# Expert matrices of a mixture-of-experts stage: two chunks of 704 columns in place of four of 352

## What is computed

```python
g, u = jnp.split(x @ w_gu[ex], 2, axis=-1)      # w_gu[ex]: 1024 x (2 * 1408)
y = (jax.nn.silu(g) * u) @ w_dn[ex]             # w_dn[ex]: 1408 x 1024
```

## Time and profile before

| | |
|---|---|
| median of three runs (lowest, highest) | 2723.92 us (2721.8, 2724.9) |
| the profiled execution, its own time | 2721.46 us |
| its span in the trace | 2719.4 us |
| PE busy over the span | 2486.5 us (91%) |
| DVE, ACT busy | 1607.8 us (59%), 1391.2 us (51%) |
| TensorE clock granted, mean | 0.96 of full |
| data moved | 472.23 MB, mean 174 GB/s |

### The profile page before, as it was taken

One profiled execution on the slowest core, in us unless ns is written; L12 is line 12 of the kernel. 1 busy time (PEld: TensorE's weight loads), 2 busy tenths in 40 slices (PEclk: granted clock), 3 DMA queues, 4 the chain that ended last, 5 costly groups with the idle time before them and its releaser, 6 DMA issues. The chain is left out here.

```text
span 2719.4 us, 52138 instructions
## 1 busy us (share of the span) xinstructions
PE 2486.5 (91%) x19059; PEld 2166.9 (80%) x19059; DVE 1607.8 (59%) x2330; ACT 1391.2 (51%) x2117; POOL 395.6 (15%) x571
## 2 busy tenths in 40 slices
PE   6998969999889999899799788888999999999993
PEld 4887958778578888788677788777999999999992
DVE  3255566665752232223311688547888888888885
ACT  4225655554323333212222566417888788787873
POOL 1133122221141000011200343042000000000002
PEclk8998989999999999999899899888999999999996
DMA  7530000000541222223254000319999999999994
GB/s 271 203 127 3 18 5 3 3 3 3 197 157 47 77 73 74 77 78 124 79 214 147 31 16 13 120 50 342 381 388 380 387 380 382 383 377 385 376 383 190
DMA packets 262845, 472.23 MB, mean 174 GB/s; under 512 B 29436, under 2 KB 202108, under 8 KB 256548
## 3 DMA queue, kind: packets, MB, share of 16 engines
q1 hardware_dynamic: 255200, 445.69, 46.5%
q0 software_dynamic: 4416, 14.70, 1.4%
q10 hardware_dynamic: 3076, 9.71, 0.9%
HBM read 453.54 MB, written 16.48 MB: 173 GB/s over the span
## 5 line engine op out<-in xcount | busy, mean ns | idle before, releaser
L3379 DVE TENSOR_TENSOR m_lo<-m_raw,m_hi 128x1408 fp32r<-128x1408 f32 (+1 forms) x459 | 648.4, 1457 | 64.8 <-ACT m_hi L3238 62.5
L3238 ACT ACTIVATE m_hi<-m_raw 128x1408 fp32r<-128x1408 f32 (+1 forms) x459 | 548.6, 1246 | 41.8 <-DMA m_raw<-moe_w_gu 27.3
L195 DVE TENSOR_TENSOR w_lo<-w_raw,w_hi 128x1024 fp32r<-128x1024 f32 (+1 forms) x132 | 162.1, 1231 | 485.3 <-ACT w_hi L190 484.7
L213 PE MATMUL acc<-w_hi,h_hi 128*128 128x512 f32 (+1 forms) x1120 | 431.9, 386 | 18.0 <-PEq L2798 9.4
L215 PE MATMUL acc<-w_hi,h_lo 128*128 128x512 f32 (+1 forms) x1120 | 424.9, 379 | 0.0
L214 PE MATMUL acc<-w_lo,h_hi 128*128 128x512 f32 (+1 forms) x1120 | 424.7, 379 | 0.0
L190 ACT ACTIVATE w_hi<-w_raw 128x1024 fp32r<-128x1024 f32 (+1 forms) x134 | 135.0, 1014 | 457.2 <-PE acc L215 401.9
L213 PEld LDWEIGHTS acc<-w_hi,h_hi 128*128 128x128 f32 x1120 | 213.1, 190 | 79.1 <-issue 33.8
L215 PEld LDWEIGHTS acc<-w_hi,h_lo 128*128 128x128 f32 x1120 | 212.9, 190 | 34.5
L214 PEld LDWEIGHTS acc<-w_lo,h_hi 128*128 128x128 f32 x1120 | 213.3, 190 | 32.6
L3156 PE MATMUL p_gates<-m_hi,x_hi 128*128 128x352 f32 x544 | 181.7, 334 | 5.0 <-issue 5.0
(11 more groups left out here) (407 smaller groups left out, 4959.8 us busy)
## 6 DMA issues: line engine op xcount, KB each, us to landing
m_raw<-moe_w_gu SPq DMA_DIRECT2D x544, 352.0 KB
m_raw<-moe_w_dn SPq DMA_DIRECT2D x187, 512.0 KB
ada_w<-ada_w SPq DMA_DIRECT2D x40, 1024.0 KB, 4.9
w_raw<-ffn_w_gu SPq DMA_DIRECT2D x88, 256.0 KB, 2.9
w_raw<-w_in_o SPq DMA_DIRECT2D x24, 512.0 KB, 5.7
w_raw<-ffn_w_dn SPq DMA_DIRECT2D x22, 512.0 KB, 3.6
w_raw<-w_in_e SPq DMA_DIRECT2D x28, 384.0 KB, 5.0
scratch_y_slots<-y_slot ACTq DMA_DIRECT2D x18, 512.0 KB, 6.3
```

Source lines behind the costliest of these rows:

```text
L195: eng.tensor_tensor(lo, self.raw_of(c, k), hi, ALU.subtract).then_inc(self.lo.sem, 1)
L213: eng.matmul(out, hi, whi[:, b, :], start=first, stop=False)
L3238: a.activation(whi[:, u % MSPLIT, 0:size(u)], raw[:, s, 0:size(u)], ACT.Copy).then_inc(s_hi.sem, 1)
L3379: dve.tensor_tensor(wlo[:, u % MSPLIT, 0:n], raw[:, u % MRAW, 0:n], whi[:, u % MSPLIT, 0:n], ALU.subtract).then_inc(s_lo.sem, 1)
```

## The change

The gate and up matrices are read in CH = 2 chunks of ECH = 704 columns. A unit is no longer gates and ups of the same columns, but gates alone or ups alone: four units of gates, then four of ups, for each chunk. The 704 columns are two pieces `q` of 352, each in its own bank, so both banks of an accumulator now belong to one chunk. A piece of a load is 704 consecutive columns (2816 bytes) in place of two runs of 352 (1408 bytes). Number of units, elements in a unit, number and width of matmuls stay.

Silu and product are done twice in a visit, on 704 columns: silu behind units 7 and 15, product behind units 11 and 19. PE waits for the silu before it begins the next chunk's gates, and for the product before its ups. The steps that hang behind units move: `turn_a` to units 10, 11, 19 and 20, AT_PART_A to (14, 15, 21, 22), AT_PART_X from 21 to 19. `turn_x` stays behind unit 16.

```diff
-ECH = 352
+ECH = 2 * 352
...
-    GU, DN = CH * KU, D_EXPERT // P
+    GU, DN = CH * 2 * KU, D_EXPERT // P
...
-    X_USES, A_USES = (3, 4), (0, 1, 2, 5)
-    AT_Y, AT_SILU, AT_PART_A, AT_PART_X = 4, (8, 12, 16, 20), (11, 15, 19, 23), 21
+    X_USES, A_USES = (2, 3), (0, 1, 4, 5)
+    AT_Y, AT_SILU, AT_ACT, AT_PART_A, AT_PART_X = 4, (7, 15), (11, 19), (14, 15, 21, 22), 19
...
+        def chunk_of(u):
+            c, r = divmod(u, 2 * KU)
+            return c, *divmod(r, KU)
...
-                            src = wgu[bass.ds(e, 1), :, 2 * k + b, :, c * ECH:(c + 1) * ECH].rearrange("e p h n -> p (e h) n")
-                            sp.dma_start(gu(raw, u)[:, b], src).then_inc(landed[s].sem, 16)
+                            src = wgu[bass.ds(e, 1), :, 2 * k + b, half, c * ECH:(c + 1) * ECH].rearrange("e p n -> p (e n)")
+                            sp.dma_start(gu(raw, u)[:, b].rearrange("p q n -> p (q n)"), src).then_inc(landed[s].sem, 16)
...
-                pe.wait_ge(s_act.sem, s_act.at(tile * CH + (c + 1)))
+                pe.wait_ge(s_act.sem, s_act.at(tile * CH + (c // 2 + 1)))
...
-                        if k == 0:
-
-                            pe.wait_ge(s_act.sem, s_act.at(tile * CH + (c - 1)))
+                        if k == 0 and half == 0:
+
+                            pe.wait_ge(s_silu.sem, s_silu.at(tile * CH + c))
+                        elif k == 0:
+
+                            pe.wait_ge(s_act.sem, s_act.at(tile * CH + c))
...
-                                pe.matmul(acc[:, c % 2, 0:ECH], xh[:, j, :], h[:, b, half, :], start=start, stop=False)
+                                pe.matmul(acc[:, q, 0:ECH // 2], xh[:, j, :], h[:, b, q, :], start=start, stop=False)
...
-                    if u in (7, 11, 15):
-                        turn_a(tile, (u - 7) // 4)
+                    if u in (10, 11):
+                        turn_a(tile, u - 10)
...
-                    if u == 19:
-                        turn_a(tile, 3)
+                    if u in (19, 20):
+                        turn_a(tile, u - 17)
...
-                        a.wait_ge(s_used.sem, s_used.at(tile * NU + 4 * (c + 1)))
+                        a.wait_ge(s_used.sem, s_used.at(tile * NU + (2 * KU * c + KU)))
...
-                        a.activation(silu[:], pG[:, c % 2, 0:ECH], ACT.Silu).then_inc(s_silu.sem, 1)
+                        a.activation(silu[:].rearrange("p (q n) -> p q n", q=2), pG[:, :, 0:ECH // 2], ACT.Silu).then_inc(s_silu.sem, 1)
...
-                    if u in AT_SILU:
-                        c = AT_SILU.index(u)
+                    if u in AT_ACT:
+                        c = AT_ACT.index(u)
                         dve.wait_ge(s_silu.sem, s_silu.at(tile * CH + (c + 1)))
-                        dve.tensor_tensor(act[:, c * ECH:(c + 1) * ECH], silu[:], pU[:, c % 2, 0:ECH], ALU.mult).then_inc(s_act.sem, 1)
+                        dve.wait_ge(s_used.sem, s_used.at(tile * NU + 2 * KU * (c + 1)))
+                        dve.tensor_tensor(act[:, c * ECH:(c + 1) * ECH].rearrange("p (q n) -> p q n", q=2), silu[:].rearrange("p (q n) -> p q n", q=2),
+                                          pU[:, :, 0:ECH // 2], ALU.mult).then_inc(s_act.sem, 1)
```

More of the change, by code:

```diff
@@ L304, in _ @@
             pe.sem_inc(K.sig("m_act").sem, 2)
+            pe.sem_inc(K.sig("m_silu").sem, 1)
             pe.sem_inc(K.sig("m_y").sem, 1)
@@ L320, in prime @@
     K.sig("m_act").base += 2
+    K.sig("m_silu").base += 1
     K.sig("m_y").base += 1
@@ L2955, in tail_stage @@
     CH, KU = D_EXPERT // ECH, J // 2
-    GU, DN = CH * KU, D_EXPERT // P
+    GU, DN = CH * 2 * KU, D_EXPERT // P
     NU = GU + DN
-    NTURN = CH + 2
     TA = ((0, 2), (2, 5), (5, 8), (8, 11))
-    X_USES, A_USES = (3, 4), (0, 1, 2, 5)
-    AT_Y, AT_SILU, AT_PART_A, AT_PART_X = 4, (8, 12, 16, 20), (11, 15, 19, 23), 21
+    NTURN = len(TA) + 2
+    X_USES, A_USES = (2, 3), (0, 1, 4, 5)
+    AT_Y, AT_SILU, AT_ACT, AT_PART_A, AT_PART_X = 4, (7, 15), (11, 19), (14, 15, 21, 22), 19
     assert NU % MRAW == 0 and NU % MSPLIT == 0
@@ L3010, in tail_stage @@
         idx = K.sb(ctx, "slot_tokens", [P, SLOT_TILES + 1], I32)
-        K.sb(ctx, "gap", [P, 1000])
+        K.sb(ctx, "gap", [P, 1000 - ECH // 2])
         tok, idx0 = K.sb(ctx, "token_ids", [P, NT], I32), K.sb(ctx, "first_tokens", [P, 1], I32)
@@ L3025, in gu @@
         def gu(ring, u):
-            return ring[:, u % ring.shape[1], :].rearrange("p (j h n) -> p j h n", j=2, h=2)
+            return ring[:, u % ring.shape[1], :].rearrange("p (j q n) -> p j q n", j=2, q=2)
+        def chunk_of(u):
+            c, r = divmod(u, 2 * KU)
+            return c, *divmod(r, KU)
         def size(u):
@@ L3063, in _ @@
                     if u < GU:
-                        c, k = divmod(u, KU)
+                        c, half, k = chunk_of(u)
                         for b in range(2):
-                            src = wgu[bass.ds(e, 1), :, 2 * k + b, :, c * ECH:(c + 1) * ECH].rearrange("e p h n -> p (e h) n")
-                            sp.dma_start(gu(raw, u)[:, b], src).then_inc(landed[s].sem, 16)
+                            src = wgu[bass.ds(e, 1), :, 2 * k + b, half, c * ECH:(c + 1) * ECH].rearrange("e p n -> p (e n)")
+                            sp.dma_start(gu(raw, u)[:, b].rearrange("p q n -> p (q n)"), src).then_inc(landed[s].sem, 16)
                     else:
@@ L3124, in turn_x @@
                 for j in range(4):
-                    mm = pe.transpose(pT[:, half ^ (0 if first else 1), j * P:(j + 1) * P], xg[:, 4 * half + j:D:J], K.ident[:])
+                    mm = pe.transpose(pT[:, half, j * P:(j + 1) * P], xg[:, 4 * half + j:D:J], K.ident[:])
                 mm.then_inc(s_turned.sem, 1)
@@ L3145, in _ @@
                     if u < GU:
-                        c, k = divmod(u, KU)
-                        if k == 0:
-                            pe.wait_ge(s_act.sem, s_act.at(tile * CH + (c - 1)))
+                        c, half, k = chunk_of(u)
+                        acc = (pG, pU)[half]
+                        if k == 0 and half == 0:
+                            pe.wait_ge(s_silu.sem, s_silu.at(tile * CH + c))
+                        elif k == 0:
+                            pe.wait_ge(s_act.sem, s_act.at(tile * CH + c))
                         pe.wait_ge(s_lo.sem, s_lo.at(tile * NU + (u + 1)))
@@ L3154, in _ @@
                             start, stop = j == 0, j == J - 1
-                            for half, acc in ((0, pG), (1, pU)):
-                                pe.matmul(acc[:, c % 2, 0:ECH], xh[:, j, :], h[:, b, half, :], start=start, stop=False)
-                                pe.matmul(acc[:, c % 2, 0:ECH], xh[:, j, :], l[:, b, half, :], start=False, stop=False)
-                            for half, acc in ((0, pG), (1, pU)):
-                                mm = pe.matmul(acc[:, c % 2, 0:ECH], xl[:, j, :], h[:, b, half, :], start=False, stop=stop)
+                            for q in range(2):
+                                pe.matmul(acc[:, q, 0:ECH // 2], xh[:, j, :], h[:, b, q, :], start=start, stop=False)
+                                pe.matmul(acc[:, q, 0:ECH // 2], xh[:, j, :], l[:, b, q, :], start=False, stop=False)
+                            for q in range(2):
+                                mm = pe.matmul(acc[:, q, 0:ECH // 2], xl[:, j, :], h[:, b, q, :], start=False, stop=stop)
                         mm.then_inc(s_used.sem, 1)
@@ L3165, in _ @@
                             pe.wait_ge(s_y.sem, s_y.at(tile + 1))
-                        for c in range(CH):
+                        for c in range(len(TA)):
                             if k == TA[c][0]:
@@ L3255, in _ @@
                         for half in range(2):
-                            part_x(use(tile, X_USES[half]), half, half ^ 1)
+                            part_x(use(tile, X_USES[half]), half, half)
             n = SLOT_TILES
@@ L3407, in _ @@
             for tile in range(1, SLOT_TILES + 1):
-                pool.wait_ge(s_turned.sem, s_turned.at(2 if tile == 1 else NTURN * (tile - 2) + 7))
+                pool.wait_ge(s_turned.sem, s_turned.at(2 if tile == 1 else NTURN * (tile - 2) + 6))
                 pool.indirect_dma_start(xg[:, :], None, K.h_rows[:, :],
```

## The result

The changed kernel takes 2733.54 us (median of 9 runs, 2729.61 to 2736.4), the kernel before 2724.9 us in the same sessions (9 runs). The ratio is 1.0032, 95% interval 1.0024 to 1.0041: slower by 8.6 us. 2735.2 us was forecast, and 11.2 us of loss.

A forecast was written before the change was run, and what follows sets the result against it. PE's stream was taken as the bound; waits of 16 x 0.69 + 0.2 = 11.2 us on the profiled 2721.46 gave 2732.7, and the median, 2.46 higher, 2735.2 us; range 2724 to 2747.

The forecast's parts named there:

- The bound: Loop of visits: PE's stream is the bound at 48.4 us a visit, with the transfers just behind it.
- the loads at nothing: Loads in the loop: same bytes in pieces twice as long, and PE doesn't wait for them; cost 0.
- rival B: Loads in the loop: transfers are the true bound, longer pieces save 3.1 us a visit; 2671 us, chance 0.04.
- C: Loads in the loop: DVE's pause of 6 us empties the queue, 25 us on top; 2760 us, chance 0.07.
- PE's work at nothing: Each visit: PE's matmuls and transposes are the same in number and width before and after; cost 0.
- Silu and product: Each visit: silu 0.74 us on ACT, product 0.88 on DVE, both ready before PE asks; cost 0.
- The last two pieces: Turn between visits: ACT's and DVE's chain takes 8.97 us, PE's six units 8.28; PE waits 0.69 us each turn.
- The restarts: PE's restart at both waits of a turn: 0.08 us each, 2.6 us in all, only in the bounds.
- The hand-over of 0.06: End of the turn's chain, between DVE's first low part and PE's first gates: about 0.06 us.
- a drain beside the table load: ACT's table load in the turn's chain: a drain of about 1380 ns would make the turn 2.07 us; not counted.
- A: Turn between visits: the chain ends 0.7 us sooner than summed, so no wait shows; 2724 us, chance 0.12.
- D: PE's clock in the loop: the new waits let it fall, 48 us on top; 2783 us, chance 0.03.

The follow-up runs named there:

- experiment 7: The kernel before with its loads in long pieces, runs of 704 columns, nothing else changed: 2725.6 us, ratio 0.9996 to the kernel before.
- experiment 4: The changed kernel with a plain copy in place of the silu, so no table loads on ACT in the loop: 2721.05 us, ratio 0.9993 to the kernel before.
- Experiment 5: The kernel of experiment 1 with the first product behind unit 13 in place of 11: 2743.1 us, ratio 1.0064 to the kernel before.
- experiment 1: The changed kernel with the third and fourth transposed pieces copied out behind units 22 and 23, not 21 and 22: 2717.54 us, ratio 0.998.
- experiments 1 to 4: Besides experiment 1 and experiment 4: changed kernel with only the fourth piece's copy moved, 2723.12 us; kernel before with only the last piece transposed and copied as changed, 2736.49 us.

## Why the prediction was right

**The bound, and the loads at nothing.** Right. PE's stream sets the visit; long pieces took ACT's waits for loads away in the kernel before and gave no time (experiment 7), so rival B is out. C is out because ACT does not wait for a load in the steady visits after. How long ACT waits for loads depends also on how early it comes: in experiment 4, with long pieces and no table loads, it waits 27.6 us for them in all, and PE is not held up by it.

**PE's work at nothing.** Wrong, and it is the one term that was put at nothing and had a size. Number and width of matmuls did stay, but the move of the buffers made gates and ups 0.3 us a visit shorter: 17 x 0.32 = 5.4 us of gain that no step of the sum had. Matmuls that come closer together were named as a sign that the sum is wrong, for rival B; they did come closer, from 0.162 to 0.160 us, but by the place of the buffers and not by the loads. I had read the buffer's size in the change for its duration and not for its address.

**Silu and product.** Summed at 0.74 and 0.88 us, measured 0.76 and 0.88. Silu over at 11.0 us after the first gates, measured 2211.09 - 2200.14 = 10.95; product at 19.5, measured 19.28. Experiment 5 shows the price beyond the spare.

**The last two pieces.** The chain of 8.97 us and PE's 8.28 came out to the hundredth, and the loss ahead of the gates at 0.69 us. The restarts, which I kept in the bounds at 0.08 for both waits and out of the sum, are 0.10 to 0.12. The one at unit 23 costs nothing by itself, since PE waits for the chain behind it anyway and the 0.69 holds it; the one at the gates comes on top and belongs in the sum: 0.81 us a turn. The last visit's down part is 17.12 us against 16.79 in experiment 1, 0.33 for its 0.2: its wait, its restart and the matmuls beside them. The hand-over of 0.06 was put in without a row; it measures 2200.14 - 2200.08 = 0.06. As to a drain beside the table load: after as before no time stands beside the 1.28 us (2195.75 + 1.28 = 2197.03, and the next conversion starts at 2197.04), and the turn costs 0.81 us, not the 2.07 that it would with the drain.

**The sum again**: 16 x 0.81 + 0.33 = 13.3, less 5.4, is 7.9 us; the loop measures 8.1, and the medians differ by 8.6. The agreement of the loop is better than it need be: the first visit, before the loop is steady, takes from 50.2 to 53.8 us in the runs that leave the first product in its place. The wait and its size were right; that the total came as near as 11.2 to 8.6 was partly luck, two errors of opposite sign: 2 us too little loss and 5.4 us of gain unseen. That the wait explains the loss is shown by experiments 1 to 4, in both directions.

**A and D.** A is out by the same runs. For D, the clock stays at 1.00 from 1862 to 2670 us with both waits in each visit. The Trainium skill (TensorE: Matmul & The Clock Gate, A second HAM failure mode: psum-queue depth-cycling) tells of a kernel whose clock oscillated with small idle times between groups of matmuls, in each iteration of a cycle through PSUM banks. Two pauses of under half a microsecond in 48.7 did not do that here, so the prediction's "just this kind" was too strong.

## What to carry to other kernels

Where one engine's stream is the bound, a change that leaves its instructions alone can only be judged by the spare time of the others at their thinnest place: write the hand-over chain at a loop's turn as a sum from two rows of each engine, and count for each moved step how much work of the bound engine lies behind it and how much of the engines that prepare its operands (the helpers). A step that waits for the bound engine holds all that is queued behind it, so put it late in the helpers' order even if its own consumer has time. And when a buffer changes size, rerun the old kernel with the shift alone before crediting the change.

## What the runs showed of the hardware that was not expected

Where the buffers lie changes the pace of the matmuls that read them: 352-column matmuls start 0.160 us apart (1.92 us for 12) with the split weights shifted by 128 or 1408 bytes, 0.162 us (1.945 for 12) with none or 256. Unit and pieces are multiples of 128 bytes (a piece of 352 columns is 5.5 times 256, a unit 22 times), so a shift by 128 exchanges which pieces lie on a 256-byte grid, and as many lie on it as before. So alignment alone doesn't explain the gain: without the shift the two matmuls that read the first piece at the start of each six are slower (0.167 for 0.160), and with it those that read the second piece are not. The down matmuls didn't change (16.37 to 16.38 us in the kernel before and its three shifted runs). Which of the moved buffers it is, and by what mechanism, wasn't tried: product, its parts and the result row moved along with the weights.

A PE wait costs about 0.1 us more than its length: the matmul behind it starts, and the next one follows only after 0.34 us for 0.23, or 0.26 for 0.16. Transposes show nearly the same: the matmul behind them has 0.32 to the next start.
